# Seven block products for eight in the up projections of two feed-forward layers, their gate products on GpSimd, and a modulation vector computed beside the down projections

## The reference, cut to what matters

```
def swiglu_ffn(x, w_in, w_down):          # layers 0 and 1; hidden width 2816
    h = x @ w_in                          # 1024 x 5632
    g, u = h[..., :FFN_HIDDEN], h[..., FFN_HIDDEN:]
    return (jax.nn.silu(g) * u) @ w_down  # 2816 x 1024

x = layer_norm(ALPHA * x + y, ln_g[i, 2], ln_b[i, 2])     # behind it

c_act = jax.nn.silu(c)                    # third block; c is 1 x 1024
mod = (c_act @ mod_w[l] + mod_b[l])       # 1024 x 6144
```

## Time and profile before

| | us |
|---|---|
| median of 3 runs | 2318.23 |
| lowest, highest | 2298.22, 2323.58 |
| span of the profiled execution | 2302.4 |
| busy: PE, VectorE, ScalarE, GpSimd | 2235.3, 1271.0, 936.0, 298.9 |
| up projection behind its first two units, layer 0 and layer 1 (20 units each) | 226.1, 217.6 |

### The profile page before, as it was taken

The page is one execution under the profiler, slowest core; times in us unless marked ns, Lnnn a source line. Parts: engine busy times, 40 slices in busy tenths (PEclk is TensorE's granted clock), DMA queues, the critical chain, the costliest instruction groups (busy, mean ns, idle before and its releaser), DMA issues.

```text
span 2302.4 us, 47528 instructions
## 1 busy us (share of the span) xinstructions
PE 2235.3 (97%) x18842; PEld 2140.7 (93%) x18846; DVE 1271.0 (55%) x2590; ACT 936.0 (41%) x1547; POOL 298.9 (13%) x318
## 2 busy tenths in 40 slices
PE   7999999999999999989999999999999998999998
PEld 7978999999999996978999999999989898999998
DVE  6477443665553256889463476554165655656513
ACT  4566354332222143478363252222144554444312
POOL 3000300200000052336120110000033002000001
PEclk9999999999999999999999999999999999999999
DMA  6333341255542221200252245553312202333221
GB/s 172 81 94 92 104 143 56 83 140 142 138 137 101 91 66 56 74 2 1 92 164 75 74 110 140 154 144 110 106 49 92 79 20 75 91 104 97 95 106 55
DMA packets 303947, 219.07 MB, mean 95 GB/s; under 512 B 34442, under 2 KB 290384, under 8 KB 303824
## 3 DMA queue, kind: packets, MB, share of 16 engines
q1 hardware_dynamic: 251856, 188.79, 27.4%
q10 hardware_dynamic: 50208, 25.69, 4.3%
q0 software_dynamic: 1760, 2.88, 0.4%
HBM read 207.58 MB, written 2.10 MB: 91 GB/s over the span
## 4 chain that ended last, share of the span: by engine, by line
PE 90%; ACT 4%; DVE 2%; POOL 2%; issue 1%; DMA 0%; DVEq 0%; SPq 0%; POOLq 0%; ACTq 0%
PE bank L714 69%; PE bank L831 5%; PE bank L940 4%; PE bank L910 2%; PE bank L1259 2%; PE bank L1039 1%; PE bank L1210 1%; PE bank L1108 1%; POOL ZS L2562 1%; PE bank L1100 1%; PE bank L1193 1%; ACT SQ L1559 1%; PE bank L1311 1%; ACT BI L1355 1%; POOL ZS L2531 1%
## 5 line engine op out<-in xcount | busy, mean ns | idle before, releaser
L714 PE MATMUL bank<-XH,WH 128*128 128x256 f32 (+1 forms) x3184 | 887.4, 279 | 6.2 <-DVE HF L2245 2.7
L714 PE MATMUL bank<-XH,WL 128*128 128x256 f32 (+1 forms) x3184 | 886.0, 278 | 0.0
L714 PE MATMUL bank<-XL,WH 128*128 128x256 f32 (+1 forms) x3184 | 886.0, 278 | 0.0
L681 DVE TENSOR_TENSOR WL<-RAW,WH 128x2048 fp32r<-128x2048 f32 x160 | 369.4, 2309 | 521.5 <-ACT WH L677 521.5
L714 PEld LDWEIGHTS bank<-XH,WH 128*128 128x128 f32 (+1 forms) x3184 | 599.0, 188 | 7.1 <-issue 4.1
L714 PEld LDWEIGHTS bank<-XH,WL 128*128 128x128 f32 (+1 forms) x3184 | 600.5, 189 | 0.0
L714 PEld LDWEIGHTS bank<-XL,WH 128*128 128x128 f32 (+1 forms) x3184 | 597.4, 188 | 0.2 <-issue 0.2
L677 ACT ACTIVATE WH<-RAW 128x2048 fp32r<-128x2048 f32 x171 | 327.5, 1915 | 584.1 <-PE bank L714 545.6
L714 PE MATMUL bank<-HH,WH 128*128 (+1 forms) x1056 | 293.4, 278 | 0.9 <-DVE HF L2245 0.9
L714 PE MATMUL bank<-HH,WL 128*128 (+1 forms) x1056 | 293.3, 278 | 0.0
L714 PE MATMUL bank<-HL,WH 128*128 (+1 forms) x1056 | 293.2, 278 | 0.0
(11 more groups left out here) (359 smaller groups left out, 3666.6 us busy)
## 6 DMA issues: line engine op xcount, KB each, us to landing
RAW<-in_ffn_w_in SPq DMA_DIRECT2D x88, 512.0 KB, 4.7
MB<-in_mod_w ACTq DMA_DIRECT2D x48, 512.0 KB, 5.0
RAW<-in_ffn_w_down SPq DMA_DIRECT2D x44, 512.0 KB, 4.0
RAW<-in_ffn_up SPq DMA_DIRECT2D x44, 512.0 KB, 4.6
RAW<-in_xa_w_kv SPq DMA_DIRECT2D x32, 512.0 KB, 4.4
RAW<-in_ffn_down SPq DMA_DIRECT2D x22, 512.0 KB, 3.9
RAW<-in_xa_w_q SPq DMA_DIRECT2D x16, 512.0 KB, 4.2
RAW<-in_xa_w_o SPq DMA_DIRECT2D x16, 512.0 KB, 4.0
```

What stands on the lines that cost most here:

```text
L681: nc.vector.tensor_tensor(WL[:, par, :], RAW[:, par, :], f32(WH[:, par, :]), ALU.subtract).then_inc(w_split, 1)
L714: mm = nc.tensor.matmul(out_ap[:, cols], l, moving, start=(start and n == 0 and k == 0), stop=(stop and n == len(parts) - 1 and k == len(o ...
```

## The change

**Up projection.** Units 2 to 21 (20 of the 22) of both layers are computed as one 2x2 block product with seven products in place of eight (the Winograd form of Strassen's scheme). The blocks are: the input's first and last 512 features, left and right 256 rows of the sequence; the weight unit's upper and lower 512 rows, gate and up columns. Seven products of 4 x 3 = 12 matmuls with 256 columns make 84 a unit. Their weight factors are the blocks 11 and 21 (`gate`), 22 (`last_block`) and four sums `t1` to `t4`, which GpSimd computes from `RAW` into `TW` (`weight_sums`); the input's four sums are made once a layer on VectorE (`XS`, split into `XSH`, `XSL`). ScalarE and VectorE split the factors into slots of `WH` and `WL`, one slot for each sum. The products meet on VectorE: `add11`, `add_common`, `add_seventh`, `add21`, `add12`, seven adds of 128x256 with one operand in PSUM. The up part gathers in `UP`, a single buffer, the gate part in `HID`; ScalarE takes Silu in two halves; GpSimd multiplies `HID` by `UP` (`gated`) for units 2 to 19, VectorE for 20 and 21.

**Down projection.** `HID` holds the unsplit hidden values. ScalarE and VectorE split two slices a unit into the ring `RH`, `RLO` (`hidden_hi`, `hidden_lo`, 128x1024 each).

**Modulation.** All 24 slices of a layer stand beside the down projection, two for each unit and four more at its end. ScalarE scales the eight blocks of a slice in place, VectorE sums them in one reduction and does the transpose and the last sum; `MB` has two buffers, and ScalarE issues the next load into one when VectorE has summed it.

The diff's core, with what the text below speaks of:

```diff
+        HID = at("HID", [P, FC, S], arena)
+        XSH = at("XSH", [P, 4 * 4, S // 2], arena + 44 * KB, F32R)
+        XSL = at("XSL", [P, 4 * 4, S // 2], arena + 60 * KB, F32R)
+        MB = at("MB", [P, 2, DC, P], arena + 44 * KB)
...
+        TW = at("TW", [P, 4, S], arena + 76 * KB)
+        UP = at("UP", [P, S], arena + 84 * KB)
+        E2 = at("E2", [P, 2, S // 2], arena + 86 * KB)
+        XS = at("XS", [P, 4 * 4, S // 2], arena + 88 * KB)
+        RH = at("RH", [P, 2, 2, S], arena + 88 * KB, F32R)
+        RLO = at("RLO", [P, 2, 2, S], arena + 96 * KB, F32R)
...
                 def unit(i, j, first, last):
                     wait_unit(name, i)
-                    pe.wait_ge(hid_split, i * 2 + (FC * f + 2))
+                    if f < 2:
+                        pe.wait_ge(ring_split, i + (11 * f + 1))
+                    else:
+                        pe.wait_ge(hid_split, i * 2 + 2)
                     slot = (UNIT0[name] + j) % 2
-                    for n in (6, 7, 0, 1, 2, 3, 4, 5) if first else range(DC):
+                    for n in ((4, 5, 6, 0, 1, 2, 3, 7) if f < 2 else (6, 7, 0, 1, 2, 3, 4, 5)) if first else range(DC):
...
+                def product(slot, xs, to):
+                    half, cols = up_slots(f, slot)
+                    w0 = cols.start
+                    for c in range(4):
+                        wh, wl = (w[:, half, w0 + P * c:w0 + P * c + P] for w in (WH, WL))
+                        xh, xl = xs[c]
+                        for m, (a, b) in enumerate(((wh, xh), (wh, xl), (wl, xh))):
+                            mm = nc.tensor.matmul(to[:, LEFT], a, b, start=(c == 0 and m == 0),
+                                                  stop=(c == 3 and m == 2))
+                    mm.then_inc(product_done, 1)
...
+                def p1(p, k):
+                    pe.wait_ge(factor_split, factors(f, "gate", p, k))
+                    if unit_no(p, k) == 3:
+                        pe.wait_ge(tile_free, TILE0[name] + 4)
+                    if unit_no(p, k) not in (2, 3):
+                        pe.wait_ge(out21, done_units(f, p, k - 2))
+                    product(SLOT["11"], x11, banks_of(k)[0])
...
+                def p6(p, k):
+                    pe.wait_ge(factor_split, factors(f, "t2", p, k))
+                    pe.wait_ge(x_sums_split, 4 * f + 2)
+                    pe.wait_ge(out11, done_units(f, p, k))
+                    product(SLOT["t2"], x_sum(2), banks_of(k)[0])
...
+                def body(p, k):
+                    p6(p, k)
+                    p1(p, k + 1)
+                    p7(p, k)
+                    p2(p, k + 1)
+                    p4(p, k)
+                    p5(p, k + 1)
+                    p3(p, k)
...
+            def mod_load(h, par):
+
+                if not isinstance(h, int) or h > 0:
+                    act.wait_ge(mod_folded, h * 2 + (par - 1))
+                act.dma_start(MB[:, par, :, :], mod_wv[:, :, bass.ds(h * (2 * P) + par * P, P)]).then_inc(mod_loaded[par], 16)
+
+            def mod_scale(h, par):
+
+                act.wait_ge(mod_loaded[par], h * 16 + 16)
+                for c in range(DC):
+                    ins = nc.scalar.activation(MB[:, par, c, :], MB[:, par, c, :], ACT.Copy, scale=CA[:, c:c + 1])
+                ins.then_inc(mod_scaled, 1)
...
+                def gate_hi(p, k):
+                    act.wait_ge(w_loaded[(u0 + k) % 2], p * 32 + LOADED[u0 + k])
+                    if unit_no(p, k) == 2:
+                        act.wait_ge(tile_ready, TILE0[name] + 2)
+                    else:
+                        act.wait_ge(product_done, products(f, "21", p, k - 1))
+                    half, cols = up_slots(f, SLOT["11"], 2)
+                    copy(WH[:, half, cols].rearrange("p (c n) -> p c n", n=P), raw_blocks(f, k)["gate"]).then_inc(factor_hi, 1)
...
+                def body(p, k, more=True):
+                    sum_hi(2, p, k + 1)
+                    keep11(p, k + 1)
+                    sum_hi(3, p, k + 1)
+                    if more:
+                        gate_hi(p, k + 2)
+                    left_silu(p, k + 1)
+                    sum_hi(4, p, k + 1)
+                    if more:
+                        sum_hi(1, p, k + 2)
+                    if unit_no(p, k) != 1:
+                        right_silu(p, k)
+                    if more:
+                        last_block_hi(p, k + 2)
+
...
+                def mods(h, last=False):
+                    for par in range(2):
+                        mod_scale(h, par)
+                        if not last:
+                            mod_load(h + 1, par)
+
+                def period(i, j):
+                    next_hi(act, down, i, j, unit_used, i + (10 * f + 1))
+                    if not isinstance(i, int) or i < 9:
+                        hidden_hi(i + 2, j + 2)
+                mods(h0)
+                period(0, 0)
+                with act.Fori(0, 4) as pair:
+                    for j in range(2):
+                        mods(pair * 2 + (h0 + 1 + j))
+                        period(pair * 2 + (1 + j), 1 + j)
+                mods(h0 + 9)
+                period(9, 9)
+                mods(h0 + 10)
+                mods(h0 + 11, True)
...
+            def mod_products(m, n, par):
+
+                dve.wait_ge(mod_scaled, m + 1)
+                nc.vector.tensor_reduce(ACC[:, :], MB[:, par, :, :].rearrange("p c n -> p n c"), AXX,
+                                        ALU.add).then_inc(mod_folded, 1)
+                dve.wait_ge(mod_folded, m + 1)
+                nc.vector.transpose(ACCT[:, :], ACC[:, :]).then_inc(mod_turned, 1)
+                dve.wait_ge(mod_turned, m + 1)
                 nc.vector.tensor_reduce(MODP[:, bass.ds(n, 1), :], ACCT[:, :].rearrange("p (b r) -> p b r", r=32),
-                                        AXX, ALU.add).then_inc(mod_step, 1)
...
+                def add_common(p, k):
+                    a, b, c = banks_of(k)
+                    dve.wait_ge(kept11, done_units(f, p, k))
+                    dve.wait_ge(product_done, products(f, "t2", p, k))
+                    nc.vector.tensor_tensor(E2[:, k % 2, :], E2[:, k % 2, :], a[:, LEFT], ALU.add).then_inc(kept_sum, 1)
+                    dve.wait_ge(kept_sum, done_units(f, p, k))
+                    if unit_no(p, k) not in (2, FC - 1):
+                        dve.wait_ge(hidden_done, done_units(f, p, k - 1))
+                    nc.vector.tensor_tensor(UP[:, LEFT], E2[:, k % 2, :], b[:, LEFT], ALU.add).then_inc(kept12, 1)
...
+                def last_block_lo(p, k):
+                    dve.wait_ge(last_hi, done_units(f, p, k))
+                    dve.wait_ge(w_sums, sums_ready(f, 4, p, k))
+                    half, cols = up_slots(f, 6 + k % 2)
+                    lo, hi = (w[:, half, cols].rearrange("p (c n) -> p c n", n=P) for w in (WL, WH))
+                    nc.vector.tensor_tensor(lo, raw_blocks(f, k)["22"], f32(hi), ALU.subtract).then_inc(w_split, 1)
...
+                def body(p, k, more=True):
+                    if unit_no(p, k) not in (1, 2):
+                        add12(p, k - 1, banks_of(k - 1)[1])
+                    sum_lo(2, p, k + 1)
+                    if unit_no(p, k) != 1:
+                        add_common(p, k)
+                        add_seventh(p, k)
+                    sum_lo(3, p, k + 1)
+                    add11(p, k + 1)
+                    if more:
+                        gate_lo(p, k + 2)
+                    if unit_no(p, k) != 1:
+                        add21(p, k, banks_of(k)[0])
+                    sum_lo(4, p, k + 1)
+                    if more:
+                        sum_lo(1, p, k + 2)
+                        last_block_lo(p, k + 2)
...
+                mods(0, 0, 2)
+                period(0, 0)
+                with dve.Fori(0, 4) as pair:
+                    for j in range(2):
+                        mods(pair * 4 + (2 + 2 * j), pair * 4 + (2 + 2 * j), 2)
+                        period(pair * 2 + (1 + j), 1 + j)
+                mods(18, 18, 2)
+                mods(20, 20, 4)
...
+            def weight_sums(f):
+
+                name = f"ffn_in{f}"
+                u0 = UNIT0[name]
+
+                def unit(p, k):
+                    r = raw_blocks(f, k)
+                    pool.wait_ge(w_loaded[(u0 + k) % 2], p * 32 + LOADED[u0 + k])
+                    for t, x, y, of in ((1, r["12"], r["11"], None), (2, r["22"], weight_sum(1), 1), (3, r["22"], r["12"], None),
+                                        (4, r["21"], weight_sum(2), 2)):
+                        if unit_no(p, k) != 2:
+                            pool.wait_ge(factor_split, factors(f, f"t{t}", p, k - 1))
+                        if of is not None:
+                            pool.wait_ge(w_sums, sums_ready(f, of, p, k))
+                        nc.gpsimd.tensor_tensor(weight_sum(t), x, y, ALU.subtract).then_inc(w_sums, 1)
+                        if t == 2 and unit_no(p, k) not in (2, 3, 4):
```

(14 more changed lines are left out.)

369 lines of the change are left out of this document (308 added, 61 removed).

## The result

Before: 2320.9 us in the median of four further runs (2298.2 to 2333.9). Changed: 2446.9 us in the median of four (2434.8 to 2487.0). The ratio is **1.0548**, 95% interval 1.0459 to 1.0637: the change makes the kernel 5.5% slower. The forecast was 2407 us with a range of 2345 to 2440, so the direction held and the time lies 40 us above it and 7 above the range.

The account below looks back on a forecast made before the run. PE was taken to bound the kernel before, and a 12.2 us VectorE-GpSimd loop the new up stage. Up stages +18.4 and +26.6, entry +5.4, modulation +1 and layer's end +38 made +89 on 2318: 2407 us, range 2345 to 2440.

Parts of the forecast that it names:

- ScalarE's period in the modulation: Down stage: two weight splits plus twice scaling, waiting for VectorE's sum and issuing the reload take ScalarE 11.3 us a period.
- entry: Start of the down projection: first weights ready 11.6 us after the last sum_lo(2), PE at 8.9; 2.7 us a layer, +5.4.
- modulation: Beside the down projection: ScalarE's period equals PE's in layer 0, is 0.4 us longer in layer 1, mostly absorbed; +1 us.
- layer's end: Last four modulation slices stand on VectorE ahead of the output adds: +17.4 us in layer 0, +20.6 in layer 1, together +38.
- the up loop: Up stage: VectorE's splits and GpSimd's rows hold each other and wait for results, giving a 12.2 us period in both layers.
- The up stages: Start, 18 periods and end of the up projection's 20 units: 244.5 us, +18.4, in layer 0; 244.2, +26.6, in layer 1.
- The start: From the end of the two ordinary units to the loop's first sum_lo(2): 16 us, 10 if little collides.
- the lag: Layer's end: how far after the last unit began ScalarE starts its remaining work, 2.1 us in layer 0, 5.3 in layer 1.
- (a): Rival, up stage: GpSimd and VectorE collisions don't happen, period 9.98 us, 2302 us in all; chance 0.12.
- (b): Rival: PE remains the bound and the tails hide, -55 us, 2263 us; chance 0.04.
- (c): Rival, up loop: GpSimd wins the port ahead of last_block_lo and register instructions add 0.3; period 13 us, 2436 us; chance 0.12.
- (d): Rival: PE's clock falls because PE pauses about 2 us in 12; over +200 us; chance 0.02.

Follow-up runs that it names:

- e6: The changed kernel with the sum of a modulation slice reading its eight terms contiguously, so summing wrong elements; 2413.0 us, ratio 1.0404 to the kernel before.
- e7: The changed kernel with GpSimd's sums and gate products cut short for all units but the loop's first, most work left out; 2353.2 us, ratio 1.0129 to before.
- e1: The changed kernel with a second buffer for the up products, so VectorE waits for the gate product of two units back; 2398.8 us, ratio 1.0407 to before.
- e5: The changed kernel with the gate product of all units on VectorE, none on GpSimd; 2392.2 us, ratio 1.0313 to the kernel before.
- e8: The changed kernel with gate product and modulation on VectorE and four modulation slices a layer moved ahead, beside xa_o; 2318.4 and 2324.4 us.
- e13: e8 with add21 moved behind the splits of t4 and t1; 2304.5 us, ratio 1.0009 to the kernel before.
- e12: e8 with add12 moved ahead of last_block_lo, into VectorE's wait for GpSimd's t4; 2292.9 us, ratio 0.9964 to the kernel before.
- e9: e8 with the split of t3 moved ahead of the PSUM adds and add21 behind the split of t1; 2372.8 us, ratio 1.028 to the kernel before.

## Why the prediction was off

**The step that failed** is ScalarE's period in the modulation: "It then waits for VectorE's sum of it (1024 elements, 1.22 like the split)". The sum reads its eight terms 512 bytes apart and takes 1.98 us. Coming twice a period, this turned a ScalarE that just kept pace with PE (11.3) into one that sets it (13.06), and it stands on the layer's end as well. I took the price from a row of equal size and did not look at how the operand lies. From PE's last up product (it ends at 722.0 and 1664.8) to the last add it is now 160.1 and 161.4 us; before, from 700.5 and 1573.9, it was 125.2 and 120.5. That is +34.9 and +40.9, where entry, modulation and layer's end together gave 20.1 and 24.3: 31.4 us too little; e6, which changes nothing but the stride, gives back 34.4. With these 34.4 the sum would have been 2441 us.

By terms: PE's first ten units of the down projection take 123.1 and 125.1 us, +10.0 and +16.3 against ten at the pace of before, where the modulation was put at +1 in all; in e6 they take 109.1 and 113.2, against 113.1 and 108.8 at that pace, and little of the loss is left. The layer's end, from the start of the last unit, costs +23.5 and +23.6, forecast 17.4 and 20.6. The entry costs 1.5 and 1.0, forecast 2.7 each.

A second sign stood in the same sentence: I found ScalarE's period equal to PE's to 0.1 us. At such a balance every error of the one price goes straight into the time, and neither the range nor a rival had a case for it.

**Right: the up loop.** 12.2 us forecast, 12.43 measured, in both layers; the difference is 9.4 us over 36 periods, from `last_block_lo` held and from the instructions between rows. Its mechanism is shown by e7 (no long rows, no loop) and e1 and e5 (the wait on the product). The up stages, counted like that, cost +21.3 and +31.1, forecast +18.4 and +26.6. The start was 18.6 us, not 16: beside GpSimd three of the input's four sums take 2.23 to 2.33 in place of 1.22, and one of their four low parts. Part of this is hidden by a term that I had not foreseen: the last of the 18 periods is 9.8 us and gives 2.7 a layer back.

**Right in kind, too small: the layer's end.** The adds begin behind the last slices and not behind PE. PE begins the last unit at 846.59 and 1790.91; the adds end 35.5 and 35.3 us later, forecast 29.4 and 32.6. The walk from ScalarE's last weight split but one (853.83) to the first add (873.77) holds, 19.9 us for 19.8; wrong is the lag at which ScalarE gets there, 7.2 us in both layers for 2.1 and 5.3. With the contiguous sum of e6 it is 5.7 and 3.9, so the stride makes 1.5 and 3.3 of it; the rest of layer 0's stays open:

```profile
853.83 1.92 ACT L767 ACTIVATE WH<-RAW 128x2048 fp32r<-128x2048 f32 x1 [2.57 <-DVE ACC L2481]
```

e8, which takes the slices away, wins 18.5 us there against the changed kernel.

**Rivals.** (a), no collisions, is refuted by the held rows above. (b) was right only as what e7 leaves. (c) had part of the truth: GpSimd does win ahead of `last_block_lo`; the 13 us did not come. (d) did not occur in the up stage: 0.99 of the clock with PE idle 1.8 us in 12.4. But at a layer's end PE now stands still for 22.8 us (22.6 in layer 1), and the granted clock is 0.50 from 866 to 884; what that costs behind it was not separated.

What stays open: ScalarE's lag at the end of layer 0, why e13's gain came, in full, and the +6.0 us outside the two layers, which is within what two executions of one kernel differ by.

## What to carry to other kernels

Price a row by how its operands lie and not by its element count alone; and where an estimate puts two engines at the same pace, treat the second one as the bound and widen the range to what its least certain row would add. A saving in the busiest engine's work is worth only what the loop through the others leaves: here 55 us of saved matmuls met a loop of held rows, a start, an end and a moved side task. In a loop of engines that hold each other, move the rows that hold nobody into waits that are there anyway, one at a time: one row moved won 0.6 us a unit (e12), two moved together lost 0.8 (e9), though one of the two alone wins 0.3 (e13).

## What the hardware showed that was not expected

- A VectorE reduction of 128x1024 elements takes 1.22 us read contiguously and 1.98 with 512 bytes between elements (48 rows each).
- A VectorE row with two SBUF inputs that starts inside a GpSimd row is held at both lengths seen: 1024 elements 2.23 to 2.33 for 1.22, 512 elements 1.79 for 0.69. A row with a PSUM input is not: in e12, 36 of the 40 second adds of `add_common` (L2578) lie wholly inside a GpSimd row and take 0.420 to 0.423 us, the four beside none 0.420 to 0.421.
- PE's pace is not a property of the layer. Before, the products were 117.8 ns apart all through layer 0 and 113.3 through layer 1, with the clock granted in full. In the changed kernel both spacings occur in either layer and change inside a stage: among layer 0's down products it is 0.118 us from 775 to 795, 0.113 from 795 to 835 and 0.118 at 857. I priced the loop's bound by layer from the two; it did not matter, since PE wasn't the bound. What sets the spacing no run here shows.
